# Constants packed into fewer loads, and the filter's first angle moved ahead of the sums of squares

## The chip, the cores and the metric

The kernel runs on 1 core of one Trainium2 chip. The metric is the device time of one execution in microseconds, the median of the runs. TensorE is called PE in the rows, VectorE DVE, ScalarE ACT, GpSimd POOL and SyncE SP.

## What is computed

One layer of a hybrid encoder on two groups of tokens (256 and 512), all in float32. The part that matters here is the start of the layer: the modulation rows come from the conditioning vectors `c`, the first normalisation from `x`, and the filter network of the long convolution from positions alone.

```python
c_act = jax.nn.silu(c)
mod = c_act @ w_ada[l] + b_ada[l]
sh1, sc1, g1, sh2, sc2, g2 = jnp.split(mod, 6, axis=-1)
h = modulate(rmsnorm(x, norm1_g[l]), sh1, sc1)      # y*(1+sc1) + sh1
proj = h @ w_in[l]                                  # q, k, v, hyena inputs, gates
...
# filter: z holds t, cos(fr*w), -sin(fr*w) for each position, 33 wide
h = jnp.sin(f1 * (z @ w1 + b1))
h = jnp.sin(f2 * (h @ w2 + b2))
h = (h @ w3).reshape(L, N_DIRS, HYENA_ORDER, HYENA_WIDTH)
...
x = x + g1 * (merged @ w_out)                       # then an MLP with squared ReLU
```

## The kernel before

Everything is kept transposed: 128 channels on the partitions and the 768 tokens of both groups along the free axis, so `x` is eight blocks `k` of 128x768. The engines' programs are written out by hand, each in one fixed order, and meet only in semaphores. A product in full precision takes three matmuls, of a high and a low part of each operand.

The weights of the projections come as tiles of 512 KB. Tile `t` is split by ACT into its high part (`split_w`, L1282) and by DVE into its low part (L1741). From the third tile on, PE runs through tile after tile (`gemm_k`, L750), and the other engines work beside it; that goes on to the end of the program. The stage before it is the one that is changed here:

- **Loads.** SP's queue carries the vectors (`vec`), the even blocks of `x`, then pieces of the modulation weights (`mod_load`, L462, 16 pieces of 512 KB, four to each group of rows) mixed with weight tiles 0 to 3. POOL's queue carries the odd blocks of `x` and the other pieces. ACT's queue carries the unit matrix (`ident`), the filter's weights (`filt_w12`), its positions (`filt_zh`, 33 rows) and the sinks.
- **Sums.** ACT squares each block of `x` (`square`, L1298), DVE adds it to `n_acc` (`norm_acc`, L1751 and L1754), and PE sums over the partitions (`norm_sum`, L816). Meanwhile PE does idle work (`warm`, L803). Then ACT takes the root (`norm_std`), DVE the reciprocal, PE spreads it over the partitions (`norm_spread`, L824) and DVE multiplies `x` by it (`norm_t`, L1783).
- **Modulation.** For each of four groups of rows PE makes eight narrow products (`mod_row`, L789), ACT copies the rows out (`mod_rows`, L1361), PE turns them (`mod_turn`, L797), and DVE adds the biases (`mod_out`, L1817 to L1820). Group g is needed for blocks 2g and 2g+1.
- **Normalised blocks.** For each block ACT applies scale and shift (`norm_h`, L1322) and takes the high part (`norm_hi`, L1328), DVE the low part (`norm_lo`, L1787). Then PE can multiply it with weight tiles 0 and 1 (`first(s, k)`, 6 matmuls each).
- **Filter network.** PE makes z @ w1 (`filt_mlp(0)`, L846). DVE reduces the angle to a turn in six passes (`arg_first`, `arg_turns`, `arg_rest`, `arg_clamp`, L1857 to L1880), ACT takes the sine (L1372), PE makes the second layer (`filt_mlp(1)`, L848), DVE reduces again and ACT takes the second sine (L1393). A sine and a square root need another table on ACT, which `ACT_TABLE_LOAD` fetches.

The order in which PE runs the stage, from the kernel:

```python
pe.wait_ge(ld_ident, 16)
turn_c()
pe.wait_ge(ld_filt, 32)
filt_mlp(0)
...
for k in range(2, KD - 1):
    pe.wait_ge(n_acc, k)
    warm(2)
norm_sum(0)
for k in range(KD):
    mod_row(0, k)
norm_spread(0)
```

Of the kernel before, what the change touches and what calls it, by code (L numbers as in the profile page):

```python
# [20 lines left out]
P = 128  # L21
# [85 lines left out]
def program(nc, a, out_T):  # L107
    with ExitStack() as ctx:
# [23 lines left out]
        def sb(name, shape, dt=F32):  # L132
# [65 lines left out]
        ident = sb("ident", [P, P])  # L198
        ones = sb("ones", [P, P])
        vT = sb("vecT", [P, V_N])  # L200
# [10 lines left out]
        fw12 = sb("filt_w12", [64, 64 + P])  # L211
# [22 lines left out]
        ld_vec, ld_ident, ld_filt, ld_w3, ld_filt2, ld_rope, ld_x2 = (  # L234
            sem(n) for n in ("ld_vec", "ld_ident", "ld_filt", "ld_w3", "ld_filt2", "ld_rope", "ld_xback"))
# [232 lines left out]
        def _(sp):  # L468
# [143 lines left out]
        def _(pool):  # L612
# [4 lines left out]
            for p in (0, 2, 3, *range(4, 4 * MODS, 2)):  # L617
                mod_load(pool, p)
# [126 lines left out]
        def _(pe):  # L745
# [54 lines left out]
            def warm(n, to=wk[:, 1024:1280]):  # L800

                for _ in range(n):
                    pe.matmul(to, ident[:], ones[:].rearrange("p (o n) -> p o n", o=1).broadcast_to([P, 2, P]),  # L803
                              start=True, stop=True)

            def turn_c():

                pe.wait_ge(cact_done, 1)
                pe.matmul(wk[0:16, 1536:1536 + P], cact[:], ident[:], start=True, stop=True).then_inc(c_turned, 1)
# [9 lines left out]
            def norm_spread(q, h=0):  # L819

                pe.wait_ge(n_rstd, 1 if q == 0 else 2 * q + h)
                for b in range(NTB) if q == 0 else blocks(h):
                    c = P * b
                    mm = pe.matmul(wk[:, c:c + P], rs[:, b:b + 1].broadcast_to([P, P]), ident[:],  # L824
# [18 lines left out]
            def filt_mlp(layer):  # L843
                for c0, L in GROUPS:
                    if layer == 0:
                        mm = pe.matmul(acc_ps[0:64, 0, c0:c0 + L], fw12[0:33, 0:64], zh[0:33, c0:c0 + L], start=True, stop=True)  # L846
# [84 lines left out]
            first(1, 0)  # L931
            mod_turn(2)
            first(0, 2)
            first(1, 1)
# [12 lines left out]
            def turn_v():  # L947
                pe.wait_ge(acc_free[T_V % 2], T_V // 2 + 1)
                pe.wait_ge(f_free, len(FU) - 1)
                for b in range(NTB):  # L950
                    mm = pe.transpose(wk[:, P * b:P * b + P], vtmp[:, P * b:P * b + P], ident[:])
# [21 lines left out]
            def turned(n):  # L973
# [21 lines left out]
            def turn(n):  # L995
                g, _, nct = UNITS[STEPS[n][0]]
                pe.wait_ge(fold_done, n + 1)
                for e in range(2):
# [8 lines left out]
                    for i, row in enumerate(rows):  # L1007
                        mm = pe.transpose(wk[:, c + P * i:c + P * i + P], row, ident[:])
# [260 lines left out]
        def _(act_e):  # L1269
            act_e.dma_start(ident[:], a["t_ident"]).then_inc(ld_ident, 16)  # L1270
            act_e.dma_start(fw12[:], a["filt_w12"]).then_inc(ld_filt, 16)
            act_e.dma_start(zh[0:33, :], a["t_z"]).then_inc(ld_filt, 16)
# [104 lines left out]
            mod_rows(1)  # L1377
            norm_h(2)
# [8 lines left out]
            norm_hi(5)  # L1387
            for k in range(6, KD):
# [346 lines left out]
        def _(dve):  # L1735
# [163 lines left out]
            arg_first(1)  # L1899
# [7 lines left out]
            arg_turns(1)  # L1907
# [623 lines left out]

def tables():
# [4 lines left out]
    out = {"t_ident": np.eye(P)}  # L2537
# [11 lines left out]
    zs = []  # L2549
    for L in (TS, TP):  # L2550
        t = np.linspace(0.0, 1.0, L, dtype=f)
        w = (f(2.0 * PI) * np.arange(L, dtype=f) / f(L)).astype(f)
        fr = np.linspace(1e-4, 15, 16, dtype=f)
        fw = (fr[:, None] * w[None, :]).astype(f).astype(np.float64)
        zs.append(np.concatenate([t[None].astype(np.float64), np.cos(fw), -np.sin(fw)], axis=0))
    out["t_z"] = np.concatenate(zs, axis=1)
# [47 lines left out]
def laid_out(inputs):  # L2604
# [25 lines left out]
    h["vec"] = np.concatenate([h["vec"], np.stack([np.concatenate([v, v]) for v in fv], 1), sel], axis=1)  # L2630
# [40 lines left out]
```

## Time and profile before

| | |
|---|---|
| median of 3 runs | 1111.06 us (1111.06 to 1111.72) |
| profiled execution, its own time | 1114.14 us |
| its span | 1112.6 us |
| PE busy | 1092.2 us, 98% |
| DVE, ACT, POOL busy | 72%, 41%, 10% |
| data moved | 138.85 MB, mean 125 GB/s |

The profile is one execution. PE is busy nearly all the time, so its few waits and the stretches in which it has little to do are what is to be read. The stage that is changed takes the first 57 us of the span.

### The profile page before, as it was taken

To read this page: it belongs to the slowest core of one execution; us is meant where nothing else is said; L and a number is where in the kernel's file an instruction comes from. 1 tells how busy PE (TensorE), PEld (TensorE's weight loads), DVE (VectorE), ACT (ScalarE), POOL (GpSimd) and SP (SyncE) were. 2 spreads that over 40 slices of the span, in tenths; PEclk is the share of its full clock that TensorE was granted. 3 is DMA by queue.
4 is the path that set the end of the run, shared out by engine and by line. 5 is a ranking of instruction groups with operands and counts; after the bars stand their busy time and mean duration, and the time that the engine had idled before them with its cause. 6 is when DMAs were issued, how large, how long until landed. Compare 5 with 4: busy or idle time off the path is not lost.

```text
span 1112.6 us, 16634 instructions
## 1 busy us (share of the span) xinstructions
PE 1092.2 (98%) x6304; PEld 1022.2 (92%) x6304; DVE 802.3 (72%) x1334; ACT 454.5 (41%) x792; POOL 108.9 (10%) x132
## 2 busy tenths in 40 slices
PE   6999999999999999999999999999999999999997
PEld 4787798888899999999899999999999999999886
DVE  5777699889388685556455777787978778788534
ACT  5631156665722322423246232253442526157414
POOL 2101200000334322000000000000000000000000
PEclk9999999999999999999999999999999999999998
DMA  9923454333332333753312331143333232222303
GB/s 345 394 86 117 154 189 143 129 127 114 119 123 105 119 104 124 282 153 108 110 57 95 125 121 57 57 152 99 111 103 106 95 109 91 87 76 76 95 19 115
DMA packets 45525, 138.85 MB, mean 125 GB/s; under 512 B 5051, under 2 KB 10635, under 8 KB 44556
## 3 DMA queue, kind: packets, MB, share of 16 engines
q1 hardware_dynamic: 29024, 80.21, 21.6%
q0 software_dynamic: 11376, 44.84, 11.3%
q10 hardware_dynamic: 5052, 12.81, 3.3%
q8 instruction: 47, 0.77, 0.3%
q14 instruction: 26, 0.21, 0.1%
HBM read 121.61 MB, written 15.74 MB: 123 GB/s over the span
## 4 chain that ended last, share of the span: by engine, by line
PE 93%; DVE 4%; DMA 1%; ACT 1%; issue 0%; ACTq 0%; DVEq 0%
PE acc_ps L750 39%; PE wk L1181 16%; PE acc_ps L1200 12%; PE acc_ps L832 12%; PE wk L1056 2%; PE acc_ps L839 1%; PE wk L991 1%; PE wk L980 1%; PE wk L970 1%; PE wk L1022 1%; PE wk L872 1%; PE wk L885 1%; DVE dot_out L1832 1%; DMA filt_zh<-in_t_z 1%; PE wk L803 1%; PE wk L890 1%
## 5 line engine op out<-in xcount | busy, mean ns | idle before, releaser
L750 PE MATMUL acc_ps<-act_hilo,w_hi 128*128 128x384 f32 x1504 | 332.5, 342 | 0.1
L750 PEld LDWEIGHTS acc_ps<-act_hilo,w_hi 128*128 128x128 f32 x1504 | 264.8, 189 | 18.8 <-issue 17.7
L750 PE MATMUL acc_ps<-act_hilo,w_lo 128*128 128x384 f32 x752 | 191.5, 335 | 0.0
L750 PEld LDWEIGHTS acc_ps<-act_hilo,w_lo 128*128 128x128 f32 x752 | 136.4, 188 | 0.0
L1200 PE MATMUL acc_ps<-hidden_hilo,act_hilo 128*128 128x384 f32 x768 | 134.6, 335 | 0.2
L1200 PEld LDWEIGHTS acc_ps<-hidden_hilo,act_hilo 128*128 128x128 f32 x768 | 133.2, 188 | 1.1 <-issue 1.1
L1741 DVE TENSOR_TENSOR w_lo<-w_raw,w_hi 128x1024 fp32r<-128x1024 f32 x61 | 76.3, 1252 | 55.1 <-ACT w_hi L1282 54.1
L1282 ACT ACTIVATE w_hi<-w_raw 128x1024 fp32r<-128x1024 f32 x61 | 64.2, 1053 | 44.3 <-PE acc_ps L750 40.9
L2198 DVE SCALAR_TENSOR_TENSOR xT<-acc_ps,modT,xT 128x512 f32<-128x512 f32 (+1 forms) x32 | 19.7, 617 | 59.7 <-PE acc_ps L832 59.5
L1832 DVE CUSTOM_DVE_ANT_0 dot_out<-dot_ring,c_rows,vecT 128x1024 f32<-128x1024 f32 x48 | 61.6, 1284 | 1.6 <-issue 0.6
L2323 DVE SCALAR_TENSOR_TENSOR xT<-acc_ps,modT,xT 128x384 f32<-128x384 f32 (+2 forms) x96 | 40.5, 478 | 28.8 <-PE acc_ps L1200 28.8
L750 PE MATMUL acc_ps<-hidden_hilo,w_hi 128*128 128x384 f32 x256 | 54.7, 334 | 0.0
L1515 ACT ACTIVATE gates_out<-acc_ps 128x768 f32<-128x768 f32 x16 | 13.0, 813 | 98.3 <-PE acc_ps L750 98.3
L832 PE MATMUL acc_ps<-hidden_hilo,w_down_hilo 128*128 128x512 f32 (+1 forms) x288 | 50.2, 336 | 0.0
L832 PEld LDWEIGHTS acc_ps<-hidden_hilo,w_down_hilo 128*128 128x128 f32 x288 | 44.4, 190 | 5.6
L1181 PE MATMUL wk<-act_hilo,w_hi 128*128 128x384 f32 x192 | 48.7, 334 | 0.0
L1181 PE MATMUL wk<-t_hilo,w_hi 128*128 128x384 f32 x192 | 48.7, 334 | 0.0
L2305 DVE TENSOR_TENSOR c_st<-wk,c_st 128x384 f32<-128x384 f32 x84 | 44.9, 551 | 2.7 <-PE wk L1181 2.3
L750 PEld LDWEIGHTS acc_ps<-hidden_hilo,w_hi 128*128 128x128 f32 x256 | 45.3, 188 | 0.0
L1614 ACT ACTIVATE act_hilo<-w_raw 128x512 fp32r<-128x512 f32 x32 | 20.0, 626 | 59.0 <-PE acc_ps L1200 59.0
L2312 DVE TENSOR_TENSOR hidden_hilo<-c_st,hidden_hilo 128x384 fp32r<-128x384 f32 x48 | 26.8, 558 | 22.5 <-ACT hidden_hilo L1633 22.2
L1605 ACT ACTIVATE w_hi<-s_sum 128x512 fp32r<-128x512 f32 x24 | 14.9, 628 | 64.1 <-DVE s_sum L2280 64.1
(301 smaller groups left out, 2026.4 us busy)
## 6 DMA issues: line engine op xcount, KB each, us to landing
w_raw<-in_w_pre SPq DMA_DIRECT2D x50, 512.0 KB, 3.5
dot_ring<-in_w_ada_cols POOLq DMA_DIRECT2D x48, 512.0 KB, 3.8
w_raw<-in_w_up SPq DMA_DIRECT2D x32, 512.0 KB, 3.7
w_raw<-in_w_down SPq DMA_DIRECT2D x16, 512.0 KB, 3.4
w_raw<-in_w_down_half SPq DMA_DIRECT2D x32, 256.0 KB, 2.7
spec<-filt_out POOLq DMA_DIRECT2D x12, 512.0 KB, 2.9
gate_spill<-gates_out ACTq DMA_DIRECT2D x16, 384.0 KB, 2.3
hy_spec<-spec SPq DMA_DIRECT2D x12, 512.0 KB, 5.6
```

What stands on the lines that cost most here:

```text
L750: mm = pe.matmul(acc_ps[:, slot, 512 * h:512 * h + HALF], w[:, k, :], src[:, x, k, HALF * h:HALF * h + HALF], start=(first and i == 0), st ...
L832: mm = pe.matmul(acc_ps[:, slot, half(h)], w_i[:, k, :], src[:, x, k, half(h)], start=(n == 0 and i == 0), stop=(n == KD - 1 and i == 2))
L1056: mm = pe.matmul(wk[:, c + o:c + o + P], w, x, start=(i == 0), stop=(i == 1))
L1181: mm = pe.matmul(st_ps(q, j), w[:, k, :], st_act(j, x, k), start=(k == 0 and i == 0), stop=(k == PK - 1 and i == 2))
L1200: mm = pe.matmul(acc_ps[:, m % 2, 512 * h:512 * h + HALF], w[:, k, :], hid[:, x, k, HALF * h:HALF * h + HALF], start=(k == 0 and i == 0), ...
L1282: act_e.activation(whi[s][:] if to is None else to[0], raw[s][:], ACT.Copy).then_inc(hi_done, 1)
L1614: act_e.activation(st_weight(ST_DOWN[m % 3])[0], quarter(m % 4), ACT.Copy).then_inc(sd_hi, 1)
L1741: dve.tensor_tensor(lo, raw[s][:], hi, ALU.subtract).then_inc(lo_done, 1)
L1832: dve.tensor_tensor_reduce(junk[:], ring[:, i], cb[:, g], 1.0, vT[:, V_BA + mt:V_BA + mt + 1], ALU.mult, ALU.add, modT[:, mt, g:g + 1]).th ...
L2305: dve.tensor_tensor(dst, st_ps(q, j), other, ALU.add).then_inc(st_u, 1)
L2312: dve.tensor_tensor(hid_block(q, b, 1), c_block(b), hid_block(q, b, 0), ALU.subtract).then_inc(h4_lo, 1)
L2323: last = dve.scalar_tensor_tensor(xT[:, m, a:b], acc_piece(s, a, b), modT[:, G2 + m, g:g + 1], xT[:, m, a:b], ALU.mult, ALU.add)
```

## The change

The unit matrix becomes 128 more columns of `vec`, on SP's queue, and `ident` is a slice of it. Positions and filter weights become one array `filt_in` of 64 rows by 960 columns, which is the first load of ACT's queue (three loads become one; the positions are now padded to 64 rows). PE runs `filt_mlp(0)` before `turn_c`, and runs `filt_mlp(1)` in the place of one `warm(2)`; the loop of warm-ups is one step shorter. Two of the eight narrow products of group 0 go ahead of `norm_sum`. DVE reduces the first angle among the first sums of squares, and begins the second one ahead of the reciprocal. ACT loads the table of sines first, then that of roots, then that of sines again, takes the sine amid the squares, and copies the rows of groups 0 and 1 ahead of splitting tiles 0 and 1. On the load queues the pieces of groups 0 and 1 go ahead of the weight tiles.

```diff
@@ sync
-            mod_load(sp, 1)
+            for p in (1, 3):
+                mod_load(sp, p)
             weights(0)
+            for p in (5, 7):
+                mod_load(sp, p)
             weights(1)
-            for p in range(5, 4 * MODS, 2):
+            for p in range(9, 4 * MODS, 2):
                 mod_load(sp, p)
@@ gpsimd
-            for p in (0, 2, 3, *range(4, 4 * MODS, 2)):
+            for p in range(0, 4 * MODS, 2):
                 mod_load(pool, p)
@@ tensor
-            pe.wait_ge(ld_ident, 16)
+            pe.wait_ge(ld_filt, 16)
+            filt_mlp(0)
+            pe.wait_ge(ld_vec, 16)
             turn_c()
-            pe.wait_ge(ld_filt, 32)
-            filt_mlp(0)
             pe.wait_ge(ones_set, 2)
-            for k in range(2, KD - 1):
+            for k in range(2, 6):
                 pe.wait_ge(n_acc, k)
-                warm(2)
+                if k == 3:
+                    pe.wait_ge(f_sin, 1)
+                    filt_mlp(1)
+                else:
+                    warm(2)
+            for k in range(2):
+                mod_row(0, k)
             norm_sum(0)
-            for k in range(KD):
+            for k in range(2, KD):
                 mod_row(0, k)
             norm_spread(0)
             mod_turn(0)
-            for k in range(4):
-                mod_row(1, k)
-            pe.wait_ge(f_sin, 1)
-            filt_mlp(1)
-            for k in range(4, KD):
+            for k in range(KD):
                 mod_row(1, k)
             first(0, 0)
             mod_turn(1)
             first(0, 1)
+            first(1, 0)
             for k in range(KD):
                 mod_row(2, k)
-            first(1, 0)
+            first(1, 1)
             mod_turn(2)
             first(0, 2)
-            first(1, 1)
@@ scalar
-            act_e.dma_start(ident[:], a["t_ident"]).then_inc(ld_ident, 16)
-            act_e.dma_start(fw12[:], a["filt_w12"]).then_inc(ld_filt, 16)
-            act_e.dma_start(zh[0:33, :], a["t_z"]).then_inc(ld_filt, 16)
+            act_e.dma_start(fin[:], a["filt_in"]).then_inc(ld_filt, 16)
...
-            act_e.activation(rs[:, 0:1], epsc[:], ACT.Sqrt).then_inc(sqrt_set, 1)
+            act_e.activation(es[:, 0, 0:1], epsc[:], ACT.Sin)
+            square(0)
+            square(1)
             act_e.wait_ge(c_turned, 1)
             ...
-            for k in range(KD):
+            square(2)
+            square(3)
+            act_e.wait_ge(f_arg, 1)
+            act_e.activation(h1[:], fb[0:64, :], ACT.Sin).then_inc(f_sin, 1)
+            for k in range(4, KD):
                 square(k)
+            act_e.activation(rs[:, 0:1], epsc[:], ACT.Sqrt).then_inc(sqrt_set, 1)
             act_e.wait_ge(sqrt_set, 1)
             norm_std(0)
-            act_e.activation(es[:, 0, 0:1], epsc[:], ACT.Sin)
+            mod_rows(0)
             split_w(0)
-            mod_rows(0)
-            split_w(1)
-            act_e.wait_ge(f_arg, 1)
-            act_e.activation(h1[:], fb[0:64, :], ACT.Sin).then_inc(f_sin, 1)
             norm_h(0)
             norm_hi(0)
             norm_h(1)
             norm_hi(1)
             mod_rows(1)
+            split_w(1)
             ...
             norm_hi(5)
+            act_e.activation(es[:, 0, 0:1], epsc[:], ACT.Sin)
@@ vector
-            for k in range(KD):
-                norm_acc(k)
             arg_first(0)
             arg_turns(0)
+            norm_acc(0)
+            arg_rest(0)
+            norm_acc(1)
+            arg_clamp(0)
+            for k in range(2, KD):
+                norm_acc(k)
+            arg_first(1)
             norm_rstd(0)
-            arg_rest(0)
-            arg_clamp(0)
+            arg_turns(1)
             norm_t(0)
             ...
             mod_out(1)
-            arg_first(1)
             split_w(1)
             ...
             norm_t(5)
-            arg_turns(1)
             norm_lo(4)
```

On DVE, at the program's start, this stood before (`n_sq` is a block of squares, `n_acc` their sum, `filt_arg`, `filt_turn` and `filt_red` the angle on its way):

```order
L1849 TENSOR_TENSOR c_padded<-c_sig,vecT 128x8x2
L1751 COPY n_acc<-n_sq 128x768
L1754 TENSOR_TENSOR n_acc<-n_acc,n_sq 128x768 x7
L1857 TENSOR_SCALAR filt_arg<-acc_ps,vecT 64x768
L1865 TENSOR_SCALAR filt_turn<-filt_arg 64x768
L1866 TENSOR_SCALAR filt_turn<-filt_turn 64x768
L1770 RECIPROCAL norm_rstd<-norm_rstd 128x6
```

and this stands there now:

```order
L1857 TENSOR_TENSOR c_padded<-c_sig,vecT 128x8x2
L1865 TENSOR_SCALAR filt_arg<-acc_ps,vecT 64x768
L1873 TENSOR_SCALAR filt_turn<-filt_arg 64x768
L1874 TENSOR_SCALAR filt_turn<-filt_turn 64x768
L1759 COPY n_acc<-n_sq 128x768
L1882 SCALAR_TENSOR_TENSOR filt_red<-filt_turn,filt_arg 64x768
L1882 SCALAR_TENSOR_TENSOR filt_red<-filt_turn,filt_red 64x768
L1762 TENSOR_TENSOR n_acc<-n_acc,n_sq 128x768
L1887 SCALAR_TENSOR_TENSOR filt_red<-filt_turn,filt_red 64x768
L1888 TENSOR_SCALAR filt_red<-filt_red 64x768
L1762 TENSOR_TENSOR n_acc<-n_acc,n_sq 128x768 x6
L1865 TENSOR_SCALAR filt_arg<-acc_ps,vecT 128x768
```

All of the first angle has moved ahead of the last six sums, and the first pass of the second angle ahead of the reciprocal.

On PE, from the program's start to the spreading of the reciprocal, this stood before:

```order
L809 MATMUL wk<-ident,c_act 16x128
L846 MATMUL acc_ps<-filt_zh,filt_w 64x512
L846 MATMUL acc_ps<-filt_zh,filt_w 64x256
L803 MATMUL wk<-ones,ident 128x256 x10
L816 MATMUL wk<-ones,n_acc 128x1 x6
L789 MATMUL wk<-mod_raw,c_padded 32x512 x8
L824 MATMUL wk<-ident,norm_rstd 128x128 x6
```

and this stands there now:

```order
L849 MATMUL acc_ps<-filt_in 64x512
L849 MATMUL acc_ps<-filt_in 64x256
L812 MATMUL wk<-vecT,c_act 16x128
L806 MATMUL wk<-ones,vecT 128x256 x2
L851 MATMUL acc_ps<-filt_h,filt_in 128x512
L851 MATMUL acc_ps<-filt_h,filt_in 128x256
L806 MATMUL wk<-ones,vecT 128x256 x4
L792 MATMUL wk<-mod_raw,c_padded 32x512 x2
L819 MATMUL wk<-ones,n_acc 128x1 x6
L792 MATMUL wk<-mod_raw,c_padded 32x512 x6
L827 MATMUL wk<-vecT,norm_rstd 128x128 x6
```

Ten warm-up matmuls have become six, the second filter product stands among them, and two narrow products stand between the last warm-up and the sum. (Each float32 matmul here is two in the trace.)

On ACT, from the rows of group 3 on, a table load now stands between the high part of block 5 and block 6:

```order
L1360 ACTIVATE mod_rows<-wk 128x512
L1331 ACTIVATE act_hilo<-n_h 128x768
L1395 ACT_TABLE_LOAD
L1395 ACTIVATE att_sinke<-eps 128x1
L1325 ACTIVATE n_h<-xT_in,modT,norm_scale 128x512
L1325 ACTIVATE n_h<-xT_in,modT,norm_scale 128x256
L1331 ACTIVATE act_hilo<-n_h 128x768
```

Before, block 6 followed block 5 there with nothing between.

## Rows read from the trace of the kernel before

**Rows 1.** The page: the span, and PE's busy time.

```profile
span 1112.6 us, 16634 instructions
PE 1092.2 (98%) x6304; PEld 1022.2 (92%) x6304; DVE 802.3 (72%) x1334; ACT 454.5 (41%) x792; POOL 108.9 (10%) x132
```

**Rows 2.** Waits of PE, 0 to 60 us: total, times, longest.

```profile
PE wk L809 <- DVE c_act L1847: 5.0, 1, 5.0
PE acc_ps L846 <- DMA filt_zh<-in_t_z: 4.1, 1, 4.1
PE wk L797 <- ACT mod_rows L1361: 1.1, 1, 1.1
```

**Rows 3.** DMA of 0 to 16 us: GB/s by slices of 0.4 us; issues with us to landing.

```profile
GB/s 0 0 0 0 24 165 304 216 292 309 286 305 265 305 359 353 340 302 294 354 331 339 254 262 270 316 310 334 363 387 401 419 417 425 440 389 443 425 410 430
...
w_raw<-in_w_pre SPq DMA_DIRECT2D x2, 512.0 KB, 17.7
...
vecT<-in_vec SPq DMA_DIRECT2D x1, 81.0 KB, 2.2
ident<-in_t_ident ACTq DMA_DIRECT2D x1, 64.0 KB, 2.4
```

**Rows 4.** Timeline of DVE, 16 to 25 us: start, duration, instructions.

```profile
16.70 2.02 DVE L1754 TENSOR_TENSOR n_acc<-n_acc,n_sq 128x768 f32<-128x768 f32 x2 [0.30 <-ACT n_sq L1298]
18.64 1.06 DVE L1857 TENSOR_SCALAR filt_arg<-acc_ps,vecT 64x768 f32<-64x768 f32 x1
19.73 0.55 DVE L1865 TENSOR_SCALAR filt_turn<-filt_arg 64x768 f32<-64x768 f32 x1
...
22.40 0.95 DVE L1874 SCALAR_TENSOR_TENSOR filt_red<-filt_turn,filt_red 64x768 f32<-64x768 f32 x1
...
24.36 0.55 DVE L1880 TENSOR_SCALAR filt_red<-filt_red 64x768 f32<-64x768 f32 x1
```

**Rows 5.** Chain that ended last, 0 to 60 us: start, us, what.

```profile
9.71 2.82 PE acc_ps L846 x4
...
19.65 1.23 PE wk L816 x12
20.88 1.85 PE wk L789 x16
22.73 1.53 PE wk L824 x12
24.27 1.03 PE wk L797 x8
...
45.29 0.79 PE wk L797 x8
46.08 14.02 PE acc_ps L750 x79
```

**Rows 6.** Busy time in windows, warm-ups alone: PE, PEld, PEclk, DMA, GB/s.

```profile
13.00:15.00 2.00, 2.00 (x6) 1.59 (x5) 1.00 1.02 417
...
18.00:19.00 1.00, 1.00 (x6) 0.90 (x5) 1.00 1.02 410
```

**Rows 7.** Timeline of ACT, 20 to 36 us.

```profile
21.26 1.28 ACT L1367 ACT_TABLE_LOAD   x1
...
25.04 0.83 ACT L1372 ACTIVATE filt_h<-filt_red 64x768 f32<-64x768 f32 x1
26.14 1.31 ACT L1322 ACTIVATE n_h<-xT_in,modT,norm_scale 128x512 f32<-128x512 f32 x2 [0.27 <-DVE norm_scale L1820]
27.48 0.84 ACT L1328 ACTIVATE act_hilo<-n_h 128x768 fp32r<-128x768 f32 x1
...
35.54 0.82 ACT L1322 ACTIVATE n_h<-xT_in,modT,norm_scale 128x512 f32<-128x512 f32 x1 [0.88 <-DVE xT_in L1783]
```

**Rows 8.** Busy time in windows: PE, PEld, DVE, ACT, POOL, PEclk, DMA, GB/s.

```profile
35.00:38.20 3.20, 2.06 (x15) 1.75 (x14) 2.34 (x4) 2.52 (x4) 0.00 (x0) 1.00 1.02 402
38.30:41.60 3.30, 3.30 (x12) 3.30 (x12) 3.00 (x7) 2.16 (x4) 2.58 (x5) 0.50 0.79 265
```

More of the change, by code:

```diff
@@ L197, in program @@
         pairs = sb("hy_pairs", [P, 1024])
-        ident = sb("ident", [P, P])
         ones = sb("ones", [P, P])
-        vT = sb("vecT", [P, V_N])
+        vT = sb("vecT", [P, V_N + P])
+        ident = vT[:, V_N:V_N + P]
         csig = sb("c_sig", [P, 16])
@@ L802, in warm @@
                 for _ in range(n):
-                    pe.matmul(to, ident[:], ones[:].rearrange("p (o n) -> p o n", o=1).broadcast_to([P, 2, P]),
+                    pe.matmul(to, ident, ones[:].rearrange("p (o n) -> p o n", o=1).broadcast_to([P, 2, P]),
                               start=True, stop=True)
@@ L808, in turn_c @@
                 pe.wait_ge(cact_done, 1)
-                pe.matmul(wk[0:16, 1536:1536 + P], cact[:], ident[:], start=True, stop=True).then_inc(c_turned, 1)
+                pe.matmul(wk[0:16, 1536:1536 + P], cact[:], ident, start=True, stop=True).then_inc(c_turned, 1)
             def norm_sum(q, h=0):
@@ L823, in norm_spread @@
                     c = P * b
-                    mm = pe.matmul(wk[:, c:c + P], rs[:, b:b + 1].broadcast_to([P, P]), ident[:],
+                    mm = pe.matmul(wk[:, c:c + P], rs[:, b:b + 1].broadcast_to([P, P]), ident,
                                    start=True, stop=True)
@@ L845, in filt_mlp @@
                     if layer == 0:
-                        mm = pe.matmul(acc_ps[0:64, 0, c0:c0 + L], fw12[0:33, 0:64], zh[0:33, c0:c0 + L], start=True, stop=True)
+                        mm = pe.matmul(acc_ps[0:64, 0, c0:c0 + L], fw12[0:33, 0:64], z_in[:, c0:c0 + L], start=True, stop=True)
                     else:
@@ L950, in turn_v @@
                 for b in range(NTB):
-                    mm = pe.transpose(wk[:, P * b:P * b + P], vtmp[:, P * b:P * b + P], ident[:])
+                    mm = pe.transpose(wk[:, P * b:P * b + P], vtmp[:, P * b:P * b + P], ident)
                 mm.then_inc(v_turned, 1)
@@ L1007, in turn @@
                     for i, row in enumerate(rows):
-                        mm = pe.transpose(wk[:, c + P * i:c + P * i + P], row, ident[:])
+                        mm = pe.transpose(wk[:, c + P * i:c + P * i + P], row, ident)
                     mm.then_inc(turn_ready, 1)
@@ L2529, in _, with positions @@
                     y_half(k - 1)
+def positions():
+    import numpy as np
+    f = np.float32
+    zs = []
+    for L in (TS, TP):
+        t = np.linspace(0.0, 1.0, L, dtype=f)
+        w = (f(2.0 * PI) * np.arange(L, dtype=f) / f(L)).astype(f)
+        fr = np.linspace(1e-4, 15, 16, dtype=f)
+        fw = (fr[:, None] * w[None, :]).astype(f).astype(np.float64)
+        zs.append(np.concatenate([t[None].astype(np.float64), np.cos(fw), -np.sin(fw)], axis=0))
+    return np.concatenate(zs, axis=1).astype(f)
 def tables():
@@ L2536, in tables @@
     f = np.float32
-    out = {"t_ident": np.eye(P)}
+    out = {}
     dist = np.arange(3 * P)[None, :] - P - np.arange(P)[:, None]
@@ L2548, in tables @@
     out["t_cos"], out["t_sin"] = cos, sin
[L2549 to L2556, printed above, removed]
     lo, hi = np.log(1e-2) / 1.5, np.log(1e-2) / 0.3
@@ L2629, in laid_out @@
     sel = np.tile(np.eye(32, 2, dtype=h["vec"].dtype), (P // 32, 1))
-    h["vec"] = np.concatenate([h["vec"], np.stack([np.concatenate([v, v]) for v in fv], 1), sel], axis=1)
+    h["vec"] = np.concatenate([h["vec"], np.stack([np.concatenate([v, v]) for v in fv], 1), sel,
+                               np.eye(P, dtype=h["vec"].dtype)], axis=1)
     w1, w2, w3 = (np.asarray(inputs[n])[0] for n in ("filt_w1", "filt_w2", "filt_w3"))
@@ L2635, in laid_out @@
     w12[:, 128:] = w2
-    h["filt_w12"] = w12
+    z = np.zeros((64, T), w1.dtype)
+    z[:33] = positions()
+    h["filt_in"] = np.concatenate([z, w12], axis=1)
     h["filt_w3"] = np.concatenate([w3, w3], axis=0)
```

20 lines of the change are left out of this document (10 added, 10 removed).

## The prediction

> **What bounds the kernel now.** I read the page first. PE is busy 1092.2 of 1112.6 us [rows 1]: whatever the first stage gives or takes reaches the end unchanged, as long as PE has work from some point on without a break. Then the waits of PE: in the first 60 us there are three, 5.0 us at the start, 4.1 us for the filter's positions, 1.1 us for a row copy [rows 2]. The chain shows the rest [rows 5]: from 9.71 us PE is hardly ever without something to do, but much of it is no real work. The group at 46.08 us is 79 projection matmuls in a row, 14.02 us; from there on nothing but PE sets the pace. Of these, 60 are what is left of tiles 0 and 1 (10 calls of `first`), 60 x 14.02/79 = 10.6 us. So one moment decides the time: the end of `mod_turn(3)`, now 46.08 us. Every microsecond by which it moves is a microsecond of the span.
>
> Two more things are to be seen. Six warm-up matmuls fill 2 us from 13 us on, and six fill 1 us from 18 us on [rows 6], although PEclk says 1.00 in both: PE works at half rate (1.2 GHz) at first and at full rate (2.4 GHz) by 18 us, after it has been busy since 9.71 us. And from 38.3 to 41.6 us PEclk is 0.50, after 3.2 us in which PE was busy 2.06 us, part of that with the tiny products of `mod_turn` [rows 8].
>
> **The change, part by part.**
>
> *Loads.* `ident` and `vec`, issued together at 0.9 us, landed after 2.4 and 2.2 us with 64 and 81 KB [rows 3]. The new first loads are 240 and 145 KB, 240 KB more in all; at about 0.3 MB a us, which the queues reach from 2.4 us on [rows 3], that is 0.8 us more. I take 4.1 us for `filt_in` and 3.5 us for `vec`. Bounds for `filt_in`: 3.3 us (as `ident`) and 9.7 us (as the positions now, [rows 2, 5]); it is near the first, since it is issued first and nothing stands before it on its queue. The pieces that overtake the weight tiles cost nothing: a tile takes about 2.6 us of a queue that has half of 410 GB/s [rows 6], so tile 1, behind three more pieces, lands about 7.7 us later than now, near 31 us (tile 0 and 1 now take 17.7 us [rows 3]). Its split on ACT comes behind `mod_rows(1)`, after 33 us by the walk below. If tile 1 were 3 us later still, `first(1, 0)` would be.
>
> *The first angle.* `filt_mlp(0)` takes 2.82 us at half rate [rows 5]: 4.1 to 6.9 us. DVE then does in one row, from [rows 4]: first pass and turns 1.09 + 2 x 0.59 = 2.3, the copy of the first square 0.6 (as a 0.55 pass), two passes 1.9, one sum 1.0, last pass and clamp 1.5, six sums 6 x 1.01 = 6.1; with two short hand-overs, 13.6 us. The sum is complete at 20.5 us. Now it is complete at 18.7 us [rows 4]. This is a loss of 1.8 us, and it no longer matters when the blocks of `x` land: DVE has become the bound of the stretch. ACT's squares wait for DVE (a square needs the sum two before it), its sine (0.83 us, [rows 7]) fits between.
>
> *PE up to the sum.* It idles from 7.4 us (behind `turn_c`) until the second sum at 13 us. The third sum is ready at 15.5 us, the sine too (the clamp ends at 14.4). From there PE does `filt_mlp(1)` and two warm-ups. At half rate `filt_mlp(1)` takes what `filt_mlp(0)` took, about 2.7, and a warm-up matmul of 256 columns about 0.43 (the narrow products pass 512 columns at full rate in 1.85/4 = 0.46 [rows 5]): 2.7 + 8 x 0.43 = 6.1 us, to 21.6 us. At full rate from 18 us on PE is there by 19.9 us. Then two narrow products 0.9 (half of 1.85, since four run at a time and these are one round), `norm_sum` 1.3, six narrow products 1.8, `norm_spread` 1.5, `mod_turn(0)` 1.0 [rows 5], and 0.4 for `mod_out(0)`: 6.9 us. So `norm_h(0)` starts at 28.5 us in the first case, at 26.8 us in the second. Now it starts at 26.14 us [rows 7]. DVE's first pass of the second angle (1.06) and its turns (1.2) lie in the waits for `norm_sum` and `norm_spread`; without that cover they would cost 2.3 us.
>
> *From `norm_h(0)` to the end of `mod_turn(3)`*, now 46.08 - 26.14 = 19.9 us. What leaves it: `filt_mlp(1)` on PE, two passes of the second angle on DVE, the sine (0.83), the split of tile 1 from before `norm_h(0)`. I walk it with 1.31 and 0.84 for a block on ACT [rows 7]. Blocks 0 and 1: 4.3. `mod_rows(1)` 0.6, turn 1.0, `mod_out(1)` 0.4: 6.4, as now. Tile 1's low part 1.2, `first(1, 0)` 1.05, `mod_row(2)` 1.85 end at 10.5; `mod_rows(2)` and the turn behind `first(1, 1)` end at 12.5; `mod_out(2)` waits for the low part of block 3 and ends at 13.4, as now: the 0.88 us that ACT lost to DVE there [rows 7] goes to `first(1, 0)` ahead of `mod_row(2)`. Then the gain: two blocks and a half 3.6, `mod_rows(3)` 0.6, turn 1.0, end at 18.5. PE has its three products done by 16.4, if it runs at full rate. Now the half-rate stretch [rows 8] makes PE the last one: 12 matmuls fill 3.3 us, where 12 x 14.02/79 is 2.1. So 18.5 for 19.9: a gain of 1.4 us, if PE keeps its full rate.
>
> *The third table load* [rows 7], 1.28 + 0.2, stands between blocks 5 and 6 on ACT. The last low part then ends near 53.5 us, and `first(0, 7)` needs it 7.4 us after `mod_turn(3)`, near 54.3 us or later. Cost zero, the cover is 0.8 us. The table of roots is loaded while PE sums.
>
> In the Trainium skill, "ScalarE: Activation LUTs", section "What ACT_TABLE_LOAD costs", a switch of tables costs a drain of 1.38 us beside the load's 1.28 us. The trace shows the 1.28 but the next activation 0.01 us behind it [rows 7]; by the page the last low part would be 1.4 us later, and the sum 0.6 us larger.
>
> **The sum.** `mod_turn(3)` ends at 26.8 + 18.5 = 45.3 us with an early full rate, a gain of 0.8; at 28.5 + 18.5 = 47.0 us with a late one, a loss of 0.9. To either comes a half-rate stretch, if there is one: PE then waits almost 2 us for the first low part (28.5 + 3.1 = 31.6, and PE is through with `mod_row(1)` by 29.9) and twice 0.7 us right behind it, more than the 1.1 us that it waited before the present stretch. Such a stretch takes 1.7 us of PE's work away; PE's other waits absorb 0 to 1 us of it. I take 1.1. The four cases: -0.8, +0.3, +0.9, +2.0.
>
> Which rate when? Now full rate comes by 18 us after work without a break from 9.7 us. In the new program such work begins at 15.5 us. So I take the late case, and lean to the stretch: +1.2 us. The sum is made against the profiled execution: span 1112.6 to 1113.8, its own time 1114.1 to 1115.3. The median of the runs lies 3.1 us below the profiled time; carried over it is 1111.06 + 1.2 = 1112.3 us.
>
> **Rivals.** A measurement of this kernel can tell about 0.2% (2.2 us) from no change.
>
> 1. *The forecast: the sums of squares are later, PE warms up later* (+0.3 to +2.0, 1111.4 to 1113.1 us). Chance 0.55.
> 2. *Faster: full rate comes early and is kept.* For it speaks that `filt_mlp(1)` and the warm-ups keep PE busy from 15.5 us on, and that the half-rate stretch of now, which alone is worth 1.2 us, hangs on a wait which goes. It decides if PE is at full rate by 18 us. -0.8, with `filt_in` landed at 3.3 us -1.6: 1109.5 to 1110.3 us. Chance 0.25. That it reaches beyond -2.2 needs a gain later than 57 us as well: 0.05 of it.
> 3. *Slower by more than 0.2%: `filt_in` lands late.* It decides from 5 us on. Every microsecond of it is one of the sum on DVE. With 6 us and late full rate: +0.9 + 1.0 (1.9 on DVE, part of it hidden behind the warm-ups at half rate) + 1.1: 1114.1 us. Against it: nothing stands before it. Chance 0.12.
> 4. *PE goes down to half rate twice or for long.* PE idles 5.5 us from 7.4 us on, and waits again near 30 us. Twice 1.7 us on top of the late start: +2.9 and more, 1114.0 us. Chance 0.05.
> 5. *The loads are the bound anyway*: DMA moves 410 GB/s from 13 us on [rows 6], and all pieces of the modulation have to pass. The last pieces are then what `mod_rows(3)` waits for, and nothing changes: 1111.1 us. Against it: PE waits for no piece now [rows 2]. Chance 0.03.
>
> The Trainium skill, "TensorE: Matmul & The Clock Gate", section "What's actually happening", says that "the default state is throttled, and activity releases the throttle". By that rule the pause of PE before 13 us speaks for rival 4 and the forecast, against rival 2; the trace agrees so far as its first stretch is slow [rows 6] and a slow one follows a pause [rows 8].
>
> **The numbers.** Predicted 1112.3 us. Range 1109.8 to 1113.8: down to most of rival 2, up to the edge of rivals 3 and 4; about 0.2 is left out. The likeliest case alone is 1111.4 to 1113.1. Faster by over 0.2% (below 1108.8): 0.06, for what I can't see behind 57 us. Slower by over 0.2% (above 1113.3): 0.17, rivals 3 and 4 with the upper edge of the forecast. Within: 0.77.
>
> **What the profile would show.** `filt_mlp(0)` starts near 4.1 us. The last sum of squares ends near 20.5 us, and DVE waits for no square. The last warm-up ends near 21.5 us, the matmuls 0.43 us apart, `norm_h(0)` starts near 28 us, and PE waits some 2 us before the first projection matmul. PEclk drops once between 31 and 42 us. `mod_turn(3)` ends between 47.0 and 48.1 us, ten calls of `first` later tile 2 starts near 58 us (now 56.5 or so), and all later rows are shifted by the same amount. I am wrong if the warm-up matmuls are 0.21 us apart from 18 us on, if `filt_in` lands after 5 us, if ACT waits at the table load, or if the rows behind 60 us don't keep the shift.

## The result, and the profile after

| | time, median (lowest to highest) | ratio to before, 95% interval |
|---|---|---|
| before | 1111.39 us (1111.01 to 1113.94, 6 runs) | |
| after | 1118.95 us (1118.27 to 1122.13, 6 runs) | 1.0068 [1.0052, 1.0084] |

The change makes the kernel 7.6 us slower. Its profiled execution took 1122.13 us with a span of 1119.7 us, the longest of its six; that of before took 1114.14 with 1112.6. So 7.1 us of the profiled difference lie in the span and 0.9 outside it.

The page after, which answers to [rows 1]. PE's busy time has grown by 2.6 us; the rest of the 7.1 us is waiting.

```profile
span 1119.7 us, 16620 instructions
PE 1094.8 (98%) x6296; PEld 1021.8 (91%) x6296; DVE 802.1 (72%) x1334; ACT 456.5 (41%) x794; POOL 108.4 (10%) x131
```

The waits of PE of 0 to 70 us, which answer to [rows 2]. The wait for the positions is now the first thing on PE, and two waits are new: 5.3 us for the second sum of squares, 2.1 us for the first low part.

```profile
PE acc_ps L849 <- DMA filt_in<-in_filt_in: 5.6, 1, 5.6
PE wk L806 <- DVE n_acc L1762: 5.3, 1, 5.3
PE acc_ps L753 <- DVE act_hilo L1795: 2.1, 1, 2.1
PE wk L800 <- ACT mod_rows L1360: 0.5, 1, 0.5
PE acc_ps L851 <- ACT filt_h L1371: 0.3, 1, 0.3
```

The two first loads, from the DMA view of 0 to 16 us (KB, us from issue to landing), beside [rows 3]:

```profile
filt_in<-in_filt_in ACTq DMA_DIRECT2D x1, 240.0 KB, 4.7
vecT<-in_vec SPq DMA_DIRECT2D x1, 145.0 KB, 3.2
```

The timeline of DVE, 5 to 26 us, beside [rows 4]. The row that I had worked out stands there piece by piece, without a wait between the pieces, but it begins at 8.45 us and the sum is complete at 15.49 + 6.26 = 21.75 us.

```profile
8.45 1.07 DVE L1865 TENSOR_SCALAR filt_arg<-acc_ps,vecT 64x768 f32<-64x768 f32 x1 [3.88 <-PE acc_ps L849]
...
15.01 0.55 DVE L1888 TENSOR_SCALAR filt_red<-filt_red 64x768 f32<-64x768 f32 x1
15.49 6.26 DVE L1762 TENSOR_TENSOR n_acc<-n_acc,n_sq 128x768 f32<-128x768 f32 x6
```

The timeline of PE, 5 to 40 us (start, duration, matmuls), beside the early part of [rows 5]:

```profile
5.59 2.82 PE L849 MATMUL acc_ps<-filt_in 33*64 33x512 f32 x4 [5.59 <-DMA filt_in<-in_filt_in]
8.34 0.61 PE L812 MATMUL wk<-vecT,c_act 128*16 128x128 f32 x2
14.26 2.05 PE L806 MATMUL wk<-ones,vecT 128*128 128x256 f32 x4 [5.32 <-DVE n_acc L1762]
16.59 2.89 PE L851 MATMUL acc_ps<-filt_h,filt_in 64*128 64x512 f32 x4 [0.28 <-ACT filt_h L1371]
19.41 3.78 PE L806 MATMUL wk<-ones,vecT 128*128 128x256 f32 x8
23.12 1.92 PE L792 MATMUL wk<-mod_raw,c_padded 128*32 128x512 f32 x4
24.97 1.50 PE L819 MATMUL wk<-ones,n_acc 128*128 128x1 f32 x12
26.41 1.91 PE L792 MATMUL wk<-mod_raw,c_padded 128*32 128x512 f32 x12
...
36.10 1.84 PE L800 MATMUL wk<-vecT,mod_rows 128*128 128x2 f32 x8
```

Here the clock can be read without a clock column: four matmuls of the narrow products take 1.92 us ahead of `norm_sum` and twelve take 1.91 us behind it. PE is at half rate up to 25 us. Eight warm-ups take 3.78 us, 0.47 each. When `norm_sum` starts at 24.97 us, the sum has been complete for 3.2 us: PE's row of warm-ups and products is what is late, no longer only DVE.

Windows of 14 to 50 us (PE, PEld, DVE, ACT, POOL, PEclk, DMA, GB/s), which answer to [rows 8] (PEclk says 1.00 before the first full-rate stretch, as it did before):

```profile
14.30:24.90 10.60, 10.32 (x20) 4.98 (x20) 7.88 (x9) 6.46 (x8) 0.00 (x0) 1.00 1.03 409
25.10:35.20 10.10, 8.00 (x64) 5.04 (x65) 6.12 (x11) 5.67 (x9) 1.06 (x2) 1.00 1.03 409
35.30:42.00 6.70, 6.70 (x28) 5.99 (x30) 4.70 (x9) 5.01 (x8) 2.62 (x5) 0.50 0.70 254
42.10:50.00 7.90, 7.90 (x58) 4.60 (x53) 3.52 (x8) 4.58 (x7) 0.67 (x2) 1.00 1.00 414
```

The half-rate stretch is there, right behind the 2.1 us wait, but 6.7 us long where it was 3.3. The timeline of ACT, beside [rows 7], and the end of the chain, beside [rows 5]:

```profile
31.28 1.30 ACT L1325 ACTIVATE n_h<-xT_in,modT,norm_scale 128x512 f32<-128x512 f32 x2 [1.34 <-DVE norm_scale L1828]
...
46.72 1.30 ACT L1325 ACTIVATE n_h<-xT_in,modT,norm_scale 128x512 f32<-128x512 f32 x2 [1.35 <-issue]
...
51.33 1.28 ACT L1395 ACT_TABLE_LOAD   x1
52.63 0.20 ACT L1395 ACTIVATE att_sinke<-eps 128x1 f32<-128x1 f32 x1
```

```profile
50.64 1.05 PE wk L800 x8
51.69 10.54 PE acc_ps L753 x60
62.23 0.09 issue
62.31 7.69 PE acc_ps L753 x43
```

`norm_h(0)` starts 5.1 us later than before, `mod_turn(3)` ends 5.6 us later (51.69 for 46.08). The 60 matmuls of `first` then take 10.54 us, as worked out, and stand in one row: the third table load has delayed nothing.

### The profile page after: what moved, and what is told of

It reads as the page before. It is cut to its first block, busy times and chain, and to the rows that moved or that the text cites. A ratio compares the mean times of both kernels' runs of the same rounds, so it can differ in the third digit from the quotient of the medians.

```text
span 1119.7 us, 16620 instructions
## 1 busy us (share of the span) xinstructions
PE 1094.8 (98%) x6296; PEld 1021.8 (91%) x6296; DVE 802.1 (72%) x1334; ACT 456.5 (41%) x794; POOL 108.4 (10%) x131
## 4 chain that ended last, share of the span: by engine, by line
PE 90%; DVE 4%; ACT 1%; issue 1%; DVEq 0%; ACTq 0%
PE acc_ps L753 39%; PE wk L1186 15%; PE acc_ps L1205 12%; PE acc_ps L835 12%; PE wk L1061 2%; PE acc_ps L842 1%; PE wk L996 1%; PE wk L888 1%; PE wk L985 1%; PE wk L975 1%; PE wk L875 1%; PE wk L1027 1%; DVE dot_out L1840 1%; PE wk L883 1%; PE wk L893 1%
```

## The experiments

Each of the eleven was timed beside the kernel before on the same chip (its medians there 1112.38, 1111.78 and 1111.85 us, for the three groups). Ratios are to the kernel before of the same group, and one thousandth is 1.1 us. They are not quotients of the two medians: for warm_gap those would give 1.0053, and the ratio is 1.0043. Where I quote an event in the trace of an experiment, it is from one execution. None of them leaves work of the reference out.

### First group: the loads alone, PE's pauses, the order of two steps

**pack_only.** The kernel before with the packed arrays and nothing else (`filt_in` lies in another part of SBUF, the order of every engine is the old one, so `turn_c` stays ahead of `filt_mlp(0)`):

```diff
-            pe.wait_ge(ld_ident, 16)
+            pe.wait_ge(ld_vec, 16)
             turn_c()
-            pe.wait_ge(ld_filt, 32)
+            pe.wait_ge(ld_filt, 16)
             filt_mlp(0)
```

> The kernel before with the packed loads alone (unit matrix behind the vectors, one filter_in block), every engine's order and the order of the pieces as before. Theory A (the loss comes from PE: no warm work before 14 us, so full rate comes at 25 us and goes again at 35 us): the packing costs nothing, since PE's work begins even earlier than at 9.7 us and goes on unbroken; 1110.5 to 1112.0 us. Theory B (the packed loads are part of the loss, since the changed kernel also lost 1.3 us behind 62 us and its own time stood 2.4 us above its span, not 1.5): 1112.5 to 1114 us, with the difference between time and span above 2 us.

Measured 1113.01 us, ratio 0.9999 [0.999, 1.0008]: nothing, as theory A said, though its reason does not hold: PE's work is not unbroken, since it waits 2.5 us for the second sum. Its profiled execution ends the stage 1.4 us earlier than that of before (`mod_turn(3)` ends at 44.70 us), because its half-rate stretch lies ahead of `norm_h(0)` and not behind it. The chain, and the window of the stretch (columns as above):

```profile
43.91 0.79 PE wk L797 x8
44.70 15.36 PE acc_ps L750 x88
```

```profile
20.50:23.80 3.30, 3.30 (x16) 1.12 (x9) 3.16 (x4) 2.67 (x5) 1.06 (x2) 0.50 1.03 411
```

It is given back at one place. These are PE's waits of 400 to 450 us, of pack_only and then of before:

```profile
PE wk L1056 <- DVE hy_prod L2088: 1.8, 1, 1.8
```

```profile
PE wk L1056 <- DVE hy_prod L2090: 0.4, 1, 0.4
```

**warm_gap** and **warm_both.** The change with six warm-ups in PE's first pause, and then with four more in its second:

```diff
             pe.wait_ge(ones_set, 2)
+            warm(6)
...
+            pe.wait_ge(m_out, 2)
+            warm(4)
             first(0, 0)
```

> The changed kernel with 6 more warm-up products (12 matmul records, 5.2 us at half rate) on PE right behind turn_c, in the pause from 9 to 14.3 us. Theory A: full rate comes by 18 to 20 us instead of 25, norm_sum starts at 21.9 us (bound by DVE's last sum) instead of 25.0, and the end comes about 3 us earlier: 1115 to 1116.5 us. Theory C (the sums on DVE, complete at 21.75 us and not 18.7, are the whole of it): PE's rate matters little, 1118 to 1119 us.

> As the one with warm-ups in the first pause, and 4 more warm-up products (1.7 us at full rate) right before first(0, 0), where PE waited 2.1 us ahead of the stretch at half rate of 6.8 us. Theory A: the granted clock stays at full rate to the end of the stage, and the end comes 1.5 to 2.5 us earlier than with the first warm-ups alone: 1113 to 1114.5 us; DVE's later sums are left as +2 to +3 us over before. Theory C: no difference to the first warm-ups alone.

Measured 1118.31 us, 1.0043 [1.003, 1.0056], and 1116.91 us, 1.0038 [1.0025, 1.0051]. In warm_gap full rate comes at 12.7 us and `norm_sum` starts at 21.73 us, with the sum; but `norm_h(0)` only gains 1.6 us (29.68), because PE falls back to half rate from 23 us on, as its windows show, and again at 33 us. In warm_both the second fall is gone. The windows of warm_gap, then those of warm_both:

```profile
23.00:26.30 3.30, 3.30 (x15) 0.86 (x14) 1.19 (x3) 0.27 (x1) 0.53 (x1) 0.50 1.03 412
26.50:33.00 6.50, 4.40 (x39) 2.76 (x37) 4.33 (x8) 4.83 (x7) 0.53 (x1) 1.00 1.03 408
33.30:39.90 6.60, 6.60 (x25) 6.60 (x24) 4.36 (x8) 4.87 (x8) 1.04 (x3) 0.50 0.76 284
```

```profile
23.70:26.90 3.20, 3.20 (x13) 0.56 (x6) 1.19 (x3) 0.13 (x2) 0.53 (x1) 0.50 1.03 410
27.10:50.00 22.90, 21.61 (x146) 15.30 (x146) 16.14 (x29) 18.04 (x27) 5.77 (x11) 1.00 0.98 378
```

From `norm_h(0)` to the end of `mod_turn(3)` warm_gap takes 20.4 us (29.68 to 50.05), as the change does, and warm_both 18.4 (29.87 to 48.31): the 6.6 us stretch costs 2.0 us. Both times lie above what theory A had given (1116.5 and 1114.5 us at most), and that of warm_gap lies in the range of theory C. Together the fills gain 3.0 thousandths on the change, which is clear of the intervals. What the second fill adds to the first, 0.5 thousandths, is not, though it takes 1.7 us off the stage in the two traces.

**rows_first.** The change with `mod_row(2)` back ahead of `first(1, 0)`:

```diff
             first(0, 1)
-            first(1, 0)
             for k in range(KD):
                 mod_row(2, k)
-            first(1, 1)
+            first(1, 0)
             mod_turn(2)
             first(0, 2)
+            first(1, 1)
```

> The changed kernel with one edit undone: the eight narrow products of group 2 stand ahead of first(1, 0) again, and first(1, 1) behind first(0, 2). In the changed kernel ACT waited 2.25 us for these products and the low part of tile 1 comes late. Theory A (PE's rate decides): mod_rows(2) comes 1.5 to 2.5 us earlier but PE then waits elsewhere; 1117 to 1118.5 us. Theory D (this order is a main part of the loss): 1115 to 1116.5 us.

Measured 1117.88 us, 1.0049 [1.0036, 1.0062]: about 2 us better than the change by the ratios, whose intervals overlap, and in theory A's range. Its profiled execution gains more, because full rate came at 22.9 us in it and stayed. That isn't the edit's doing: up to there it runs the change's program, which got full rate at 25.1 us. So I repeated the edit on two other bases below. Free of half rate from `norm_h(0)` on, it shows what the rest of the stage takes with the angle moved and this order as before:

```profile
30.14 1.30 ACT L1325 ACTIVATE n_h<-xT_in,modT,norm_scale 128x512 f32<-128x512 f32 x2 [1.34 <-DVE norm_scale L1828]
```

```profile
47.53 12.63 PE acc_ps L753 x71
```

That is 17.4 us (30.14 to 47.53), where pack_only, also at full rate there, takes 18.4 (26.32 to 44.70).

### Second group: one part alone, and one part undone

**angle_back.** The change with the first angle behind the sums again (DVE's order, the first passes of the second angle too, ACT's tables and sine, PE's `filt_mlp(1)` and five times `warm(2)` as before; loads, order of pieces, the two early narrow products and the rest of the change kept):

```diff
+            for k in range(KD):
+                norm_acc(k)
             arg_first(0)
             arg_turns(0)
-            norm_acc(0)
+            norm_rstd(0)
             arg_rest(0)
-            norm_acc(1)
             arg_clamp(0)
```

> The changed kernel with the filter's first angle behind the sums of squares again (DVE, ACT with its tables, filt_mlp(1) and five warm-ups on PE as before); the packed loads, the order of the pieces, two narrow products ahead of the sum, rows ahead of the splits and first(1, 0) ahead of group 2 stay. Theory A (the angle's move makes the loss, by DVE's late sums and PE's pause): tile 2 starts within 1.5 us of before's 56.5 us, 1111.5 to 1113.5 us where before has 1112. Theory D (the orders of rows, splits and first(1, 0) are as much of it): 1114.5 us or more.

Measured 1115.03 us, 1.0026 [1.0017, 1.0036]: 4.2 thousandths better than the change, clear of both intervals. Both theories hold in part: tile 2 starts at 56.95 us, as A said, and the time is that of D. `norm_h(0)` starts at 25.32 us, earlier than before. But PE then waits 1.6 us for tile 1's low part ahead of `first(1, 0)`, and PEclk is 0.50 from 34.5 to 37.7 us:

```profile
PE acc_ps L753 <- DVE w_lo L1748: 1.6, 1, 1.6
```

**angle_only.** pack_only with the angle's move on all three engines (with it the first passes of the second angle, the third table load, four warm-ups fewer, and `filt_mlp(0)` ahead of `turn_c`), and every other order as before:

```diff
             for k in range(2, 6):
                 pe.wait_ge(n_acc, k)
+                if k == 3:
+                    pe.wait_ge(f_sin, 1)
+                    filt_mlp(1)
+                else:
+                    warm(2)
```

> The packed loads and the move of the angle (DVE, ACT's tables, filt_mlp(1) in a warm-up's place), with every other order as before. Theory A: most of the loss is here: 1116 to 1118 us. Theory D: 1113 to 1115 us.

Measured 1118.06 us, 1.0058 [1.0039, 1.0077]. The move of the angle, with what belongs to it, costs 6.4 us alone. Here `filt_in` landed at 4.6 us, 0.9 earlier than in the change, and still PE's two waits of 5.3 and 2.1 us are there:

```profile
PE wk L803 <- DVE n_acc L1757: 5.3, 1, 5.3
PE acc_ps L846 <- DMA filt_in<-in_filt_in: 4.6, 1, 4.6
PE acc_ps L750 <- DVE act_hilo L1790: 2.1, 1, 2.1
```

**pack_queues.** pack_only with the new order of the modulation's pieces on SP and POOL, the engines as before:

```diff
-            mod_load(sp, 1)
+            for p in (1, 3):
+                mod_load(sp, p)
             weights(0)
+            for p in (5, 7):
+                mod_load(sp, p)
             weights(1)
```

> The packed loads and the new order of the pieces on SP's and POOL's queues, every engine's order as before. Tile 1 then lands near 29.5 us instead of 23.5, and ACT splits it before the first sine and norm_h(0), which started at 26.1 us. If that wait bites, norm_h(0) starts at 31.4 us and the end comes 4 to 5 us later (1116 to 1117 us); this is the price that the changed kernel avoids by its new place for the split. If it did not, 1112 us.

Measured 1122.45 us, 1.009 [1.0077, 1.0103]. Tile 1 comes late, as I had worked out, and here ACT splits it ahead of `norm_h(0)`, as the kernel before does. ACT's waits of 20 to 45 us:

```profile
ACT w_hi L1283 <- DMA w_raw<-in_w_pre: 7.5, 2, 6.1
```

So the order of the pieces costs 10 us unless the split moves too, twice the 4 to 5 us that I expected: `norm_h(0)` starts at 32.35 us (31.4 expected), but PE waits 5.9 us for the sine, and PEclk is 0.50 from 31.0 to 44.6 us. The change moves the split, and ACT has no such wait there.

**no_warm.** The kernel before without its ten warm-up matmuls:

```diff
             for k in range(2, KD - 1):
                 pe.wait_ge(n_acc, k)
-                warm(2)
             norm_sum(0)
```

> The kernel before without its ten warm-up products. Theory A (PE's rate is worth microseconds here): norm_sum starts at 18.8 us as DVE allows, but at half rate; full rate comes only after 22 us and the end comes 1.5 to 3 us later: 1113.5 to 1115 us. Rival: PE has waits enough in this stage to hide its half rate, 1112 us.

Measured 1114.18 us, 1.0022 [1.0013, 1.0031]. This prices half rate without any delay of DVE. The timeline of its PE shows `norm_sum` and the narrow products at half rate, where [rows 5] has 1.23 and 1.85 us:

```profile
18.20 2.69 PE L816 MATMUL wk<-ones,n_acc 128*128 128x1 f32 x12 [6.11 <-DVE n_acc L1753]
20.82 3.64 PE L789 MATMUL wk<-mod_raw,c_padded 128*32 128x512 f32 x16
```

`norm_h(0)` starts at 27.56 us, 1.4 later than before. Full rate, once there (24.8 us), lasts through the stage, so that it takes 18.4 us more to the end of `mod_turn(3)` (45.95). In the profiled execution of before that end comes at 46.08 us, for its half-rate stretch; the 2.2 thousandths are to all runs of before.

### Third group: the repairs together

**all_pe** is warm_both with the edit of rows_first; **back_rows** is angle_back with it; **pack_warm** is pack_only with a `warm(3)` behind `filt_mlp(0)`:

```diff
             pe.wait_ge(ones_set, 2)
+            warm(3)
             for k in range(2, KD - 1):
```

> The changed kernel with both fills of warm-up products (6 in the first pause, 4 ahead of first(0, 0)) and with group 2's narrow products ahead of first(1, 0) again: what PE could do for itself is done, DVE's late sums stay. Theory A plus D (three prices: DVE's late sums 3 us, PE's half rate, the order of first(1, 0)): what is left is DVE's share less what the later part saves, 1113 to 1115 us where before has 1112, and 1.5 to 2.5 us below the two fills alone. If the order is worth nothing once PE is at full rate, it equals the two fills alone (+4.2 us).

> The changed kernel with the first angle behind the sums and group 2's narrow products ahead of first(1, 0) again; packed loads, order of the pieces, two narrow products ahead of the sum, and rows ahead of the splits stay. The one with the angle alone put back was 2.9 us over before, with PE waiting 1.6 us for the low part of tile 1 and ACT 2.8 us for the rows of group 2. Theory D (that is the order of first(1, 0)): 0 to 1 us over before, 1112 to 1113 us. Rival (it comes from the pieces' order: tile 1 lands at 29.5 us): still 2 us or more over.

> The kernel before with the packed loads, and 3 more warm-up products (2.6 us at half rate) in the pause of 2.5 us that PE has there ahead of the second sum, since its filter product now starts at 5.3 us. If PE's work without a break from 5.3 us on brings full rate by 14 us in every run and keeps it, the stage ends 1.5 us earlier; but at 434 us PE waits for a table load of the filter spectra (1.77 us with the packed loads alone, 0.40 before), so 0 to 1 us of it stays: 1111 to 1112 us. Rival: nothing, 1112 us, as with the packed loads alone.

Measured: all_pe 1115.2 us, 1.0025 [1.0015, 1.0036]; back_rows 1112.95 us, 1.0011 [1.0002, 1.002]; pack_warm 1113.4 us, 1.0005 [0.9996, 1.0014]. The edit of rows_first is worth 1.3 thousandths on warm_both and 1.5 on angle_back, 1.9 on the change: 1.4 to 2.1 us each time, always the same way, though in each pair the intervals overlap. In the chain of all_pe `mod_turn(3)` ends at 46.27 us, 17.4 us after `norm_h(0)` (28.90), where warm_both took 18.4, so the trace gives the edit 1.0 us at full rate:

```profile
45.48 0.79 PE wk L800 x8
46.27 13.89 PE acc_ps L753 x78
```

The 1.0 us by which `norm_h(0)` starts earlier than in warm_both (29.87) is another matter: `filt_in` happened to land 1.0 us earlier (4.68 for 5.71 us).

No version beats the kernel before. By the ratios pack_only and pack_warm equal it; pack_warm's median of 1113.4 us is above the 1111 to 1112 expected, and its full rate was not kept, with PEclk at 0.50 from 21.2 to 24.4 us. back_rows, too, reaches tile 2 1.2 us ahead of the profiled execution of before (55.32 for 56.53 us), which has a half-rate stretch there that back_rows has not, and it, too, waits 1.8 us for `hy_prod` near 434 us.

## Why the prediction was wrong

It gave 1112.3 us, the range ended at 1113.8, and 1118.95 us were measured. The sign of the forecast and its two mechanisms (DVE's sums later, PE's full rate later) were right. **The step that failed is PE's rate.** The forecast took the late case ("So I take the late case, and lean to the stretch"), with half-rate warm-ups until 21.6 us. But then it took every following term from rows at full rate, from "two narrow products 0.9" on, and it priced the half-rate stretch at 1.1 us. In the trace full rate comes at 25.1 us, the two products take 1.9 us, and the stretch lasts 6.7 us and costs 2.0. Rival 4, half rate twice or for long, came nearest; it had a chance of 0.05 and a price of 2.9 us. The condition of rival 3, `filt_in` late, came true as well. Point by point:

- **The loads.** 4.1 us taken for `filt_in`, landed at 5.6; 3.5 for `vec`, landed at 4.1. In the DMA view of the change some 0.8 MB (my sum of its slices) have moved by 5.6 us, and these two loads are 0.385 of it: the bandwidth estimate left out what else is under way, the first blocks of `x`. The landing also differs from one execution to the next: the same load at the head of the same queue lets PE start at 5.32 us in rows_first and at 4.68 in all_pe. 1.5 us of error here, of the size that rival 3 named; 1.25 of it is left in the sum on DVE (21.75 for 20.5 us).
- **DVE's row.** 13.6 us from `filt_mlp(0)`'s end: 8.4 to 21.75 is 13.3. Right. The sum is 3.0 us later than before, not 1.8.
- **PE up to the sum.** The sine was late by 1.1 us with it, `filt_mlp(1)` and four pairs of matmuls took 6.5 for 6.1 us; the two early narrow products, 0.9 us in my sum, took 1.9 at half rate, and from `norm_sum` to `norm_h(0)` 6.3 us passed for 6.0. So `norm_h(0)` started at 31.3, 2.8 us after my late case.
- **From `norm_h(0)` to `mod_turn(3)`.** 18.5 us at full rate was right: warm_both, which has no half rate in it, takes 18.4. But my comparison was crooked. The 19.9 us of before hold its half-rate stretch: pack_only, same order without one, takes 18.4 (26.32 to 44.70). So my "gain of 1.4 us" was only the absence of a stretch that I then added again at 1.1. The stretch cost 2.0 us, since it lasted 6.7.
- **`first(1, 0)` ahead of `mod_row(2)`.** I had it absorbed in "the 0.88 us that ACT lost to DVE". The walk of 18.5 us holds this order and came true with it, so it is no part of the miss, but it is a part of the loss. With the old order rows_first and all_pe take 17.4 us: the lighter DVE and ACT do gain 1.0 us over the 18.4 of pack_only, and `first(1, 0)` gives it back, since `mod_row(2)` feeds ACT and behind `first(1, 0)` it comes later. ACT waited 2.2 us for those rows in the change. The microsecond has the size of one piece of the chain of before, the first pass of the second angle, which the moved angle takes along:

```profile
32.31 1.08 DVE filt_arg L1857
```

- **Table loads.** Cost nothing, as said. By the Trainium skill, "ScalarE: Activation LUTs", section "What ACT_TABLE_LOAD costs", a drain of 1.38 us goes with each; the trace shows none here: the load starts at 51.33, 0.01 us behind the activation ahead of it, the next activation starts at 52.63, 0.02 us behind the load's end, and nothing is lost in the chain.
- **Order of pieces, the copy of rows ahead of the split.** No run has them alone. back_rows, which has both with the split moved, is 1.1 thousandths [0.2, 2.0] over before, and that bounds what they can cost.
- **"All later rows are shifted by the same amount"** held from 62 to 378 us (5.8 us). A wait near 434 us then takes 0.75 for 0.4 us, and later ones 1.0 more, to the span's 7.1. The wait of 0.8 us is in all six kernels that have the angle moved and in none of the others, however early the stage ends.
- **Outside the span.** The time exceeds the span by 1.5 us before and by 1.9 to 2.7 in the change's six executions. It isn't PE's pause: angle_only has the same one and 1.5 to 1.8. In rows_first, which differs from the change in one order on PE, two runs have 1.7 and three 2.4 to 2.6 us. This part, about 1 us, stays unexplained.

So the miss adds up, in the profiled execution (8.0 us over before, 1.2 forecast): weighing the four cases instead of taking the last one 0.8; the late load 1.1; PE's rate 2.2 (0.4 in the warm-ups' row, 1.0 in the two products, 0.8 in the stretch); 0.3 between `norm_sum` and `norm_h(0)`; 1.5 in the rows behind the stage, and 0.9 outside the span. PE's rate is the largest term of the stage, but a third of the miss lies behind it, where the prediction had taken the shift as constant.

How the loss adds up, by the ratios: the change 6.8 thousandths; PE's pauses filled −3.0 (warm_both); the two steps swapped back −1.3 (all_pe); the angle behind the sums −1.4 (back_rows, which needs no extra warm-ups); left 1.1. Of these steps only the first is clear of its intervals (half-widths 0.9 to 1.6). In the other direction the angle alone brings 5.8 and the rest without it 2.6, more than the 6.8 together; the intervals allow both. That the moved angle is the largest part is shown from both sides: it alone costs 5.8 ± 1.9, and taking it out of the change gives back 4.2, with an interval of about ± 1.9 by my working. How its part divides between PE's rate and DVE's sums is less sure, since warm-ups also bring stretches of their own: PE's pauses filled gives 3.0, and what only the angle's return brings 1.4. How the last thousandth divides I can't say.

That the packed loads are free is measured; why their 1.4 us is lost at 434 us is only narrowed down. The 512 KB loads of `hy_spec` before it are issued 1.6 us earlier in pack_only (415.25 for 416.81) and take 6.0 for 5.2 us to land. pack_warm issues them at 415.80 us, waits 0.4 us as before does, and its span of 1111.7 us keeps 0.9 us. What holds them was not tried.

## What to carry to other kernels

Price the steps behind a moved wait at the clock that the engine will have there, and first list each stretch in which PE will have nothing to do: filling two pauses with idle matmuls was worth 3 us of the 7.6, with the same real work. Before a stretch is called a gain, take the clock's share out of the time of before, or the same microseconds are counted twice. Work that is moved into a "free" place ahead of a sum delays all that counts on this sum: the first angle had stood in waits of DVE that cost nothing. And a shift of one stage is not simply handed on: 2.4 of the 8.0 us in the profiled execution came behind the stage.

## What the runs showed of the hardware

- Full rate came at very different times: 17.8 us in the kernel before, with PE busy from 9.7; 25.1 in the change, with PE busy from 14.3; 22.9 in rows_first, whose program is the same up to there; 24.8 in no_warm; 12.7 in warm_gap.
- Seven kernels had full rate by 14 us. In six of them (the three with the first pause filled, warm_gap, warm_both and all_pe, and also pack_only, pack_warm and pack_queues) a half-rate stretch of 3.3 us then began between 20.5 and 23.7 us, on `norm_sum` or what follows it, although no single wait of PE between the two was above 1.3 us. The seventh, angle_back, kept full rate until 34.4 us. In the six that got full rate later (17.3 to 27.3 us) no such stretch came there. So early warm-ups bought less than I expected (1.6 us of 3.2).
- The clock's stretches are a large part of the spread of a kernel's runs. Each run has a span and a mean granted clock. Of the 64 runs of the kernel before that were timed beside the experiments, the 39 with a clock of 0.997 or 0.998 have a mean span of 1110.2 or 1110.1 us, the 22 with 0.996 one of 1112.1, the 3 with 0.995 one of 1112.7. In warm_gap the run at 0.997 spans 1113.9 us and the three at 0.993 span 1117.2 to 1118.2. The mean does not hold all: no_warm's ten runs at 0.997 or 0.998 span 1111.8 to 1113.9 us. Only the profiled executions show where a stretch lies. That of before (0.996) has one of 3.3 us, and 39 of 64 runs have a higher mean clock, so it was probably the wrong one of the two kinds to take for the median.
